# Two visits fewer per pair: low-rank products join the scores, probabilities times values join the intra-chunk products

## The reference, cut to what matters

```python
s = einsum('bnqhgd,bnkhd->bnhgqk', qb, kband) * ATT_SCALE
p = sink_softmax(s, sinks)
o = einsum('bnhgqk,bnkhd->bnqhgd', p, vband)
w_log = -softplus(-(w0 + tanh(dw) @ w2)) - 0.5
a = sigmoid(a0 + da @ a2)
g = sigmoid(dg) @ g2
bonus = sum(rh * kh * r_k, axis=-1, keepdims=True) * vh
```

## Time and profile before

| what | value |
|---|---|
| median of 3 runs | 3486.8 us (3486.75 to 3487.79) |
| profiled execution, its own time | 3487.86 us |
| its span | 3486.0 us |
| PE busy | 3311.1 us (95%) |
| DVE busy | 1841.0 us (53%) |
| ACT busy | 1308.5 us (38%) |
| POOL busy | 512.8 us (15%) |
| granted TensorE clock, mean | 0.987 |

### The profile page before, as it was taken

One profiled execution on the slowest core, in us unless ns is written; L12 is line 12 of the kernel. 1 busy time (PEld: TensorE's weight loads), 2 busy tenths in 40 slices (PEclk: granted clock), 3 DMA queues, 4 the chain that ended last, 5 costly groups with the idle time before them and its releaser, 6 DMA issues. The chain is left out here.

```text
span 3486.0 us, 66257 instructions
## 1 busy us (share of the span) xinstructions
PE 3311.1 (95%) x28123; PEld 2752.3 (79%) x28123; DVE 1841.0 (53%) x2943; ACT 1308.5 (38%) x2334; POOL 512.8 (15%) x413
## 2 busy tenths in 40 slices
PE   6988889998999999998999999999999999999998
PEld 4766678876777777876777787998767678989998
DVE  3455554447656465356566446325666644553334
ACT  3333343334434343344434334324444432332222
POOL 1011121013111012013112003002112111110000
PEclk9999999999999999999999999999999999999999
DMA  3211143232222254332222235232111123432222
GB/s 104 88 59 41 41 140 95 90 105 69 70 65 72 88 172 136 92 103 79 62 69 72 81 122 185 86 114 93 56 50 55 59 81 123 130 101 87 88 89 81
DMA packets 120820, 313.08 MB, mean 90 GB/s; under 512 B 17232, under 2 KB 21968, under 8 KB 120528
## 3 DMA queue, kind: packets, MB, share of 16 engines
q1 hardware_dynamic: 120528, 308.85, 28.0%
HBM read 282.80 MB, written 26.10 MB: 89 GB/s over the span
## 5 line engine op out<-in xcount | busy, mean ns | idle before, releaser
L672 PE MATMUL PS<-hh,wh 128*128 128x512 f32 (+1 forms) x3200 | 1071.9, 368 | 26.7 <-POOL hl L1330 7.7
L672 PE MATMUL PS<-hl,wh 128*128 128x512 f32 (+1 forms) x3200 | 1027.0, 353 | 0.0
L672 PE MATMUL PS<-hh,wl 128*128 128x512 f32 (+1 forms) x3200 | 1025.3, 353 | 0.0
L1038 ACT ACTIVATE wh<-raw 128x512 fp32r<-128x512 f32 x944 | 592.7, 630 | 1144.9 <-PE PS L672 1099.0
L1400 DVE TENSOR_TENSOR wl<-raw,wh 128x512 fp32r<-128x512 f32 x944 | 678.4, 721 | 564.4 <-ACT wh L1038 550.4
L672 PEld LDWEIGHTS PS<-hh,wh 128*128 128x128 f32 x3200 | 564.4, 189 | 142.0 <-issue 39.5
L672 PEld LDWEIGHTS PS<-hh,wl 128*128 128x128 f32 x3200 | 564.4, 189 | 84.7
L672 PEld LDWEIGHTS PS<-hl,wh 128*128 128x128 f32 x3200 | 566.2, 189 | 79.7 <-issue 8.8
L672 PE MATMUL PS<-fh,wh 128*128 128x512 f32 (+1 forms) x880 | 296.8, 370 | 20.1 <-POOL fl L1313 16.1
L1313 POOL TENSOR_TENSOR fl<-acc,fh 128x512 fp32r<-128x512 f32 (+1 forms) x88 | 116.6, 1325 | 1153.7 <-ACT fh L1102 1153.7
L672 PE MATMUL PS<-fl,wh 128*128 128x512 f32 (+1 forms) x880 | 283.5, 355 | 0.0
(11 more groups left out here) (244 smaller groups left out, 4067.4 us busy)
## 6 DMA issues: line engine op xcount, KB each, us to landing
raw<-w SPq DMA_DIRECT2D x384, 512.0 KB, 3.5
raw<-w SPq DMA_DIRECT2D x160, 256.0 KB, 2.8
gate_scratch<-gst SPq DMA_DIRECT2D x48, 256.0 KB, 2.0
gb<-gate_scratch SPq DMA_DIRECT2D x24, 512.0 KB, 5.2
xin<-x SPq DMA_DIRECT2D x32, 256.0 KB, 5.1
xres<-x SPq DMA_DIRECT2D x24, 256.0 KB, 3.8
y<-xres SPq DMA_DIRECT2D x24, 256.0 KB, 5.2
gate_scratch<-gst SPq DMA_DIRECT2D x16, 272.0 KB, 2.0
```

Of the source, the lines that this page charges most:

```text
L672: mm = pe.matmul(PS[:, bank(t) + f, 0:t.cols], wt[:, cols], mov[:, m, f * t.cols:f * t.cols + t.cols], start=(first and a == 0), stop=(n = ...
L1038: act.activation(wh[h % 4][:], src, ACT.Copy).then_inc(hi_done, 1)
```

## The change

S and ZA become one visit, SZ: the low-rank products follow the scores at once. PTR becomes PB and is followed by BO. PV becomes the first part of the visit PL, whose second part is the old LM without its warm-up products and without its wait for `ath`; the result of PV goes to bank 3 instead of bank 7. On DVE `bv` now stands ahead of `atl`. Weights and inner points change with it: 24 entries that sum to 56.8 become 22 that sum to 54.8.

```diff
-VISITS = (("S", 1.0), ("ZA", 1.5), ("KG", 8.0), ("PTR", 3.0), ("PV", 2.0), ("BO", 3.0), ("LM", 4.0), ("XT", 3.5),
+VISITS = (("SZ", 2.0), ("KG", 8.0), ("PB", 2.5), ("BO", 3.0), ("PL", 5.0), ("XT", 3.5),
...
-        s += ["at", "rt", "pc", "btE", "btO", "ktE", "ktO", "atl", "bv"]
+        s += ["at", "rt", "pc", "btE", "btO", "ktE", "ktO", "bv", "atl"]
...
-    s = ["s", "vt", "z", "a", "kn", "g", "ptr", "pv", "bo"]
+    s = ["s", "vt", "z", "a", "kn", "g", "ptr", "bo", "pv"]
```

TensorE:

```diff
-                yield pr.t("S")
+                yield pr.t("SZ")
...
-                yield pr.t("ZA")
                 pe.wait_ge(lor, 2 * (b + 1))
...
-                yield pr.t("PTR")
+                yield pr.t("PB")
                 pe.wait_ge(V, pr.at("V", "pn"))
...
-                yield pr.t("PV")
-                pe.wait_ge(A, pr.at("A", f"ptr{pr.chs[-1]}"))
-                for c in pr.chs:
-                    for kv in range(2):
-                        r = half_rows(kv)
-                        out = PS[r, 7, 256 * c:256 * c + 256].rearrange("p (a w) -> p a w", a=4)
-                        mm = pe.matmul(out, vtk[:, c, r], ptk[:, c, :, r], start=True, stop=True)
-                step("pv")
-                mm.then_inc(Tn, 1)
...
-                yield pr.t("LM")
-                warm()
+                yield pr.t("PL")
+                pe.wait_ge(A, pr.at("A", f"ptr{pr.chs[-1]}"))
+                for c in pr.chs:
+                    for kv in range(2):
+                        r = half_rows(kv)
+                        out = PS[r, 3, 256 * c:256 * c + 256].rearrange("p (a w) -> p a w", a=4)
+                        mm = pe.matmul(out, vtk[:, c, r], ptk[:, c, :, r], start=True, stop=True)
+                step("pv")
+                mm.then_inc(Tn, 1)
+
                 pe.wait_ge(V, pr.at("V", "bv"))
-                pe.wait_ge(A, pr.at("A", "ath"))
```

ACT, POOL and DVE (the operations are the same; what moves is their tag, and `atl` behind `bv`):

```diff
-                yield pr.t("S", 0.3)
+                yield pr.t("SZ", 0.3)
                 act.wait_ge(G, pr.at("G", "kk"))
...
-                yield pr.t("S", 0.5)
+                yield pr.t("SZ", 0.4)
...
-                yield pr.t("ZA", 0.3)
+                yield pr.t("SZ", 0.5)
...
-                yield pr.t("PTR", 0.3)
+                yield pr.t("PB", 0.3)
...
-                yield pr.t("PV", 0.4)
+                yield pr.t("PL", 0.2)
                 act.wait_ge(Tn, pr.at("T", "pv"))
...
-                yield pr.t("LM", 0.5)
+                yield pr.t("PL", 0.6)
...
-                yield pr.t("PV", 0.8)
-                dve.wait_ge(A, pr.at("A", "ath"))
-                tt_("atl", atl[:, :, pr.c0:pr.c0 + W].rearrange("p a (c w) -> p a c w", c=n),
...
                 yield pr.t("BO", 0.4)
                 dve.wait_ge(Tn, pr.at("T", "bo"))
                 own("ktO")
                 tt_("bv", v4(kt), q4(5, W), xs(8), ALU.mult)
+                yield pr.t("PL", 0.35)
+                dve.wait_ge(A, pr.at("A", "ath"))
+                tt_("atl", atl[:, :, pr.c0:pr.c0 + W].rearrange("p a (c w) -> p a c w", c=n),
...
-                yield pr.t("LM", 0.3)
+                yield pr.t("PL", 0.5)
```

More of the change, by code:

```diff
@@ L1227, in pair_steps @@
                     go(f"ptr{c}", ptk[:, c].rearrange("p a w -> p (a w)"), PS[:, 3 + c, :], ACT.Copy)
-                yield pr.t("PV", 0.4)
+                yield pr.t("PL", 0.2)
                 act.wait_ge(Tn, pr.at("T", "pv"))
                 go("ath", ath[:, :, pr.c0:pr.c0 + W].rearrange("p a (c w) -> p a c w", c=n),
-                   PS[:, 7, 0:256 * n].rearrange("p (c a w) -> p a c w", c=n, a=4), ACT.Copy)
+                   PS[:, 3, 0:256 * n].rearrange("p (c a w) -> p a c w", c=n, a=4), ACT.Copy)
                 def flat2(t):
@@ L1351, in xs @@
                     return rw[:, first:first + 4, pr.c0:pr.c0 + W]
-                yield pr.t("S", 0.1)
+                yield pr.t("SZ", 0.1)
                 pool.wait_ge(Tn, pr.at("T", "s"))
@@ L1608, in c4 @@
                     return t.rearrange("p (c a) -> p c a", a=4)
-                yield pr.t("S", 0.4)
+                yield pr.t("SZ", 0.4)
                 dve.wait_ge(Tn, pr.at("T", "s"))
@@ L1690, in pair_steps @@
                     tt_("kt" + "EO"[par], slots(r, 1 - par), both(kt, r), both(ip, r), ALU.mult)
-                yield pr.t("PV", 0.8)
-                dve.wait_ge(A, pr.at("A", "ath"))
-                tt_("atl", atl[:, :, pr.c0:pr.c0 + W].rearrange("p a (c w) -> p a c w", c=n),
-                    PS[:, 7, 0:256 * n].rearrange("p (c a w) -> p a c w", c=n, a=4),
-                    ath[:, :, pr.c0:pr.c0 + W].rearrange("p a (c w) -> p a c w", c=n), ALU.subtract)
                 yield pr.t("BO", 0.4)
@@ L1699, in pair_steps @@
                 tt_("bv", v4(kt), q4(5, W), xs(8), ALU.mult)
+                yield pr.t("PL", 0.35)
+                dve.wait_ge(A, pr.at("A", "ath"))
+                tt_("atl", atl[:, :, pr.c0:pr.c0 + W].rearrange("p a (c w) -> p a c w", c=n),
+                    PS[:, 3, 0:256 * n].rearrange("p (c a w) -> p a c w", c=n, a=4),
+                    ath[:, :, pr.c0:pr.c0 + W].rearrange("p a (c w) -> p a c w", c=n), ALU.subtract)
                 def q8(bank_, r=slice(0, 128), c0=0, width_=CH):
                     return PS[r, bank_, c0:c0 + 4 * width_].rearrange("p (a w) -> p a w", a=4)
-                yield pr.t("LM", 0.3)
+                yield pr.t("PL", 0.5)
                 for c in pr.chs:
```

## The result

| kernel | median, us | runs | ratio to before, 95% interval |
|---|---|---|---|
| before | 3487.8 (3486.75 to 3494.01) | 5 | |
| after | 3507.6 (3502.91 to 3508.81) | 5 | 1.0049 [1.0034, 1.0063] |

The change costs 20 us by the medians, where no change was forecast and the range ended at 3496; by the ratio it is 17, between 12 and 22. The profiled execution has a span of 3506.8 us, 20.8 longer than before, with a mean granted clock of 0.981 instead of 0.987. The 20.8 us are 13.0 in which TensorE is busy (3324.1 instead of 3311.1), with 16 instructions fewer, and 7.8 in which it is idle. (After's lines: L769 is `ptr`, L777 BO, L785 the product from `ptk`, L796 LM, L804 XT's tiles, L717 the warm-ups.)

The account below looks back on a forecast made before the run. TensorE, busy 95% of the span, was taken as the bound; b = 0 -2.5, b = 1 and 2 -2.2 each and b = 3 +3.5 gave -3.4 us, a median of 3483.4, range 3472 to 3496.

Parts of the forecast that it names:

- Where the visits go: All pairs: LM's products come 5 quanta earlier in b = 1 and 2; instructions can stand behind ones awaiting later quanta.
- Seams: Merging S with ZA and PV with LM saves 0.25 us per pair (bounds 0 and 0.34), 2.0 in b = 1 and 2.
- The vector queue at LM: `bv` ahead of `atl` saves 0.6 us per waiting LM; b = 0 in all -2.4 - 1.2 - 1.0 + 2.1.
- Behind PL: Late `lm` on DVE adds waits: 2.0 us at XT in pair 7, 0.7 in pair 6, 1.4 and 1.5 in 13 and 15.
- Pairs 5 and 9: Last `hl` 1.1 us later, but `fl` done at 842.5, not 846.5: 4.3 won per pair, bounds 1 and 7.
- The sum: b = 0 -2.5, b = 1 and 2 -2.2 each, b = 3 +3.5: together -3.4 us, no change; chance 0.40.
- (a): Rival, slower: `lm` collides in DVE's queue between PL and XT, +11 us, 3498; chance 0.22.
- (b): Rival, faster: pairs 5 and 9 lose wait and low clock, `e` in time, b = 0 upper bounds: -17 us, 3469; chance 0.25.
- (c): Rival: fewer visits give no time, the chain sets b = 0 and b = 3: +3 us, 3490; chance 0.13.

Follow-up runs that it names:

- e1: The changed kernel with weights and inner points that put each step at its old quantum: 3487.1 us, ratio 0.9998 to before.
- e3: The changed kernel with `ath`, `atl`, `lm`, `yd`, `yo` and `pt` placed early in PL: 3477.4 us, ratio 0.9973 to before.
- e4: The changed kernel with unused products in TensorE's waits in b = 0 and b = 3: 3501.0 us, ratio 1.0039 to before.
- e5: e3 plus unused products in TensorE's waits in b = 0 alone: 3468.9 us, ratio 0.9946 to before.
- e7: The kernel before, 24 visits, with only the points of `lm`, `yd` and `yo` moved earlier in LM: 3479.0 us, ratio 0.9972 to before.

## Why the prediction was wrong

**Where the visits go.** Right: the collisions that it named in pairs 5, 7, 13 and 15 are in the trace, and BO waits nowhere in b = 1 and 2.

**Seams.** Right in kind, 0.17 instead of 0.25. Where no wait stands in the way, pair 4 takes 0.17 us less than before in e1 and e3, pair 6 0.19 less in e3; that is for both merges together. The Trainium skill (TensorE: Matmul & The Clock Gate, Part 2: What happens when you issue a matmul) says that one matmul's drain overlaps the next one's fill; the prediction's strict reading of it, no cost at a seam, is off by this 0.17, my size by half of it. In the changed kernel a wait of 0.22 at XT in pair 4 hides even that.

**The vector queue at LM.** The waits came about as said: `bv` a slot sooner, the wait of pair 0 moved to BO (3.91 for 4.61), 24.6 for 25.5 in all. The term failed all the same. It priced the group of b = 0 by its waits alone, -2.4 - 1.2 - 1.0 + 2.1, and took the low level for a small gain in pair 1. The stretch has 21 us more at 1.2 GHz and came out at +5.8, 8.3 from the forecast. e4 recovers more than all of it without moving anything.

**Behind PL.** The waits were right: pair 7 waits 2.61 (2.0), pair 6 0.61 (0.7), KG 0.54 (0.4). In pairs 13 and 15 the wait was sized at +1.4 and +1.5 and came out at +1.1 and +2.9, and the rate of what follows was left out: b = 3 came to +11.2 instead of +3.5, with 24 us more at the low level. e3 takes the collisions away, and b = 3 comes to -1.3.

**Pairs 5 and 9.** The last `hl` is late by 1.7 (1.1 expected): the norm plane did run in 0.74 instead of 1.76, as argued. `fl` ends at 851.37 - 5.7 = 845.7, not 842.5. The step that failed is the one that took the end of the `wl` ahead of `lm` over from the kernel before, "held by its DMA" at 835.57: its `wh` now waited for a quantum behind PL, and it ended at 844.20 - 5.7 = 838.5, 2.9 later. The pairs won 2.0 and 1.6, inside the bounds of 1 and 7, under the 4.3 taken.

**The sum.** -3.4 against +20.8, 24.2 apart. Of these, 16.0 stand in b = 0 (8.3) and b = 3 (7.7), and the step that failed there is the one that turned waits into time: idle time was counted at its length, and the rate of the work behind it put at nothing but for 1.0 in pair 1 and a part of the 4.3 in pairs 5 and 9. The waits grew by 8 us over the whole kernel; about twice that, up to 20, came as busy time at the low level. The other 8.4 stand in b = 1 and 2, which have no more low-level time than before: there it is the sizes, 5.0 of it in pairs 5 and 9, with their late `wl`, the rest the seams and the waits at XT. Of the rivals, (a) had the place in DVE's queue, the sign and the low level behind waits, but put +10.6 in pairs 5 and 9, which won, and 1 us per wait for the clock, which cost some 20 in all. (b) named the right lever: `e` and `lm` in time bring 3477, but the change had them late. (c) was right in its first half: fewer visits give no time.

**What stays open.** Why the clock of b = 0 falls. It is shown that places decide it (e1 restores it) and that filled waits restore it (e4, e5). That it falls because idle time is gathered at BO is not shown, and two runs speak against it: e1 waits 11.4 us at BO, with 23.5 in all at BO, LM and XT, and has 27 us at the low level; e7 gathers nothing at BO, waits 22.9 us at its three places, and has 44. The length of the waits does not tell it either. I did not try waits of the same length spread otherwise. My items, +8 of waits and +20 of clock, exceed the +20.8 by 7 us; of these the warm-ups taken out (0.61 in four pairs) and the seams explain 4 to 5, and part of the low-level time is idle and costs nothing.

## What to carry to other kernels

When visits are merged, keep apart what the merge does and where it puts things: a kernel with the merge at the old places costs one run and here settles the question. The points at which a helper engine takes its turn were worth 30 us, where the seams gave 0.17 per pair; look for the instruction in a queue that waits for a quantum behind it. And read the granted clock by stretch beside the waits: a wait on TensorE costs its length and then, where the level falls, half of the busy time that follows; unused products in it can keep the level, at no cost as far as the wait covers them (b = 0) and at their full length where it does not (b = 3 of e4).

## What was not expected of the hardware

- The same idle time costs differently. With 25.5 us of waits at three places the first block had 27 us at the low level; with 24.6 at two, 48; with most of it filled, 13 to 16. Neither length nor number of the waits explains it: with 22.9 at three places (e7) it had 44.
- DVE's scalar-tensor-tensor on 128x512 took 1.76 us beside POOL's `hl` and 0.74 when POOL was idle, in the same pair of the two kernels.
